# Row sums of the modulations and wide sums for the first token half of the norms, in a one-core transformer kernel

## The chip, the cores and the metric

The kernel runs on one core of one Trainium2 chip, as one launch. The metric is the time of that launch on the device in microseconds. Below, TensorE is the matmul engine (PE in the rows, with PEld for its weight loads), VectorE is DVE, ScalarE is ACT, GpSimd is POOL, and SyncE is SP. PSUM is the memory that TensorE writes to, in eight banks of 128 partitions by 512 fp32 numbers; SBUF is the memory that all else works in.

## The reference

Two blocks, one behind the other, each of depth 2, on 512 tokens of 1024 numbers. Everything is fp32.

```python
# first block, layer 0 and 1
x = x + mixer(rms_norm(x, norm_mix))             # recurrence + mLSTM, then attention in a window
x = x + conv_ffn(rms_norm(x, norm_ffn), ...)     # up 1024 -> 2 x 3072, convolution of 3 taps, gelu, down
x = x + sigmoid(rms_norm(x, norm_ple) @ gate) * (p @ proj)

# second block, layer 0 and 1
mods = (silu(c) @ ada_w[i] + ada_b[i]).reshape(B, 3, 3, D_MODEL)
h = rms_norm(x, g) * (1 + mods[:, s, 1]) + mods[:, s, 0]
x = x + 0.5 * mods[:, 0, 2] * swiglu(h)          # s = 0
x = x + mods[:, 1, 2] * mixer(h)                 # s = 1
x = x + 0.5 * mods[:, 2, 2] * swiglu(h)          # s = 2
out = rms_norm(x, final_g)

def rms_norm(x, g):
    return x * rsqrt(mean(x * x, axis=-1) + EPS) * g
```

Two things of it matter here. The modulations `mods` are a product of one row `silu(c)` with a weight of 1024 by 9216 for each of the two layers of the second block: 144 columns of 128 numbers in all. And there are 13 norms, each of which needs a sum of squares over the 1024 numbers of every token.

## The kernel before

**Layout.** The residual `X` is kept in SBUF with the 1024 numbers on eight tiles of 128 partitions and the 512 tokens along the row. A matmul in fp32 leaves two records of PE and two of PEld in the trace. The feed-forward products are done by a scheme with seven half-size products in place of eight (parts P1 to P7, each 128 partitions by 256 tokens), for which GpSimd prepares sums of weight blocks (`weight_sums_of`, four operations of 128x512 for each tile) and VectorE sums of inputs and of results. Weights come through a ring of three tiles, loaded by SP.

**What sets the order.** Each engine's instructions are written out in program order by a function of its own (`@block.tensor`, `@block.vector`, ...), with waits on semaphores between them; there is no scheduler. An engine works its list strictly from the front.

**Norms.** The norms 1 to 12 are done in two token halves (`half0` is the columns 0 to 255, `half1` the rest), so that the next product can begin on the first half while the last tile of the residual is still being updated. For each half: ScalarE squares the tiles of the residual, VectorE adds the squares of the tiles 0 to 5 into `RB` (named rstd in the rows), and the squares of the tiles 6 and 7 stay in `SQ`. `half_sum` on TensorE then uses 128x128 blocks of these squares as the stationary operand and a matrix of two columns as the moving one: six matmuls of two columns, which leave the sums of 256 tokens as two columns over 128 partitions. ScalarE takes the root of 128x2 numbers (`half_root`), VectorE the reciprocal (`half_rstd`), and `half_spread` on TensorE turns and spreads them by two matmuls of 128 columns, so that a PSUM bank holds each token's factor in all partitions. VectorE multiplies residual, gain and that bank into `H` (`half_scaled`, L2440), four tiles, then the update of the last tile, then four more. In the norms 6 to 11 ScalarE adds a shift (`shifted`). Norms 1, 4, 6, 8, 9 and 11 stand ahead of a feed-forward, 3, 7 and 10 ahead of a mixer, 2 and 5 ahead of the gate, and 12 is the last.

**Modulations.** They are computed far ahead of their use, beside the two feed-forwards of the first block (`up1`/`down1` and `up4`/`down4`, the CONVOLVED ones), 24 groups of 384 numbers in each. ScalarE's queue loads a group's weights (`ada_load`, two buffers), VectorE adds eight scaled pieces of 128x384 into a sum (`ada_half`, L2488; three buffers `ada_sum`), TensorE sums it over the partitions (`ada_group`), and VectorE adds the bias and puts three columns away (`columns`, L2463). 16 groups lie beside `up`, and eight beside `down`, two in each quarter of it.

```python
            def ada_group(g):
                pe.wait_ge(S("ada_summed"), g + 1)
                if g:
                    pe.wait_ge(S("ada_taken"), g)
                for j in range(3):
                    mm(ada_columns(g)[:, j:j + 1], ada_sum(g)[:, j * P:(j + 1) * P], const("ones")[:, 0:1], True, True,
                       S("ada_full") if j == 2 else S("ada_column"))
```

So each group is three matmuls of one column, with 128x128 of the sum as the stationary operand, and a group's product waits until the columns of the one before it were taken.

## Time and profile before

| what | value |
|---|---|
| median of 3 runs | 4083.51 us (4082.96 to 4084.88) |
| the profiled execution, its own time | 4074.79 us |
| its span, first to last instruction | 4073.0 us |
| TensorE busy | 3982.9 us, 98% of the span |
| VectorE busy | 1996.8 us, 49% |
| GpSimd busy | 1338.4 us, 33% |
| ScalarE busy | 694.1 us, 17% |
| mean granted TensorE clock | 0.993 of full |

The profiled execution is 8.7 us shorter than the median of the runs. Its durations are used below, and a difference worked out from them is taken off the median as it stands. In a timeline row the first number is the start in us from the span's start, the second the time to the end of the last of the merged instructions; the starts of neighbouring rows of one engine therefore give what a stretch costs better than the durations, since matmuls overlap.

### The profile page before, as it was taken

The page shows a single profiled execution, that of the slowest core. Times are in us where ns is not written, and L with a number is a line of the kernel's source. Part 1 is how long each engine was busy: PE and PEld are TensorE (multiplying, and loading weights), DVE is VectorE, ACT ScalarE, POOL GpSimd, SP SyncE. Part 2 cuts the span into 40 slices and gives each one's busy share as a digit, 9 for nine tenths or more (in the row PEclk, how much of TensorE's full clock was granted, in tenths as well). Part 3 has the DMA queues.
Part 4 walks back from the last instruction along what each step waited for, and adds up shares of the span by engine and source line. Part 5 has one row for each costly group of instructions (what it writes and reads, how often), then busy time and mean ns, then how long its engine had stood idle before and what let it go on. Part 6 is the DMA issues. An engine that isn't in the chain of part 4 may idle for free. (4 is left out here: it accounts for less than half of the span.)

```text
span 4073.0 us, 46434 instructions
## 1 busy us (share of the span) xinstructions
PE 3982.9 (98%) x18322; PEld 3064.3 (75%) x18322; DVE 1996.8 (49%) x3654; ACT 694.1 (17%) x1506; POOL 1338.4 (33%) x1138
## 2 busy tenths in 40 slices
PE   9999999998999999999999999999999989999999
PEld 4458888754588887888854588888888647858888
DVE  5537667448476763433245443324433754444333
ACT  2321110123211101200024310001001331221000
POOL 0004444203344341344403434444443043024443
PEclk9999999999999999999999999999999999999999
DMA  3115444210245442222210122222222132112222
GB/s 132 42 57 197 165 176 151 100 67 32 83 167 181 148 176 73 86 90 80 85 68 32 42 83 93 81 95 82 84 88 88 62 113 71 35 59 83 90 81 78
DMA packets 134216, 386.87 MB, mean 95 GB/s; under 512 B 38928, under 2 KB 47248, under 8 KB 124272
## 3 DMA queue, kind: packets, MB, share of 16 engines
q1 hardware_dynamic: 116912, 301.03, 22.5%
q10 hardware_dynamic: 16272, 79.90, 5.2%
q8 instruction: 147, 2.41, 0.2%
q0 software_dynamic: 816, 2.97, 0.2%
q14 instruction: 69, 0.57, 0.0%
HBM read 375.26 MB, written 8.39 MB: 94 GB/s over the span
## 5 line engine op out<-in xcount | busy, mean ns | idle before, releaser
L954 PE MATMUL bank<-normed,weight_ring 128*128 128x256 f32 (+1 forms) x3600 | 1012.0, 435 | 4.0 <-ACT normed L1868 1.6
L954 PEld LDWEIGHTS bank<-normed,weight_ring 128*128 128x128 f32 x3600 | 676.7, 189 | 294.3 <-issue 222.9
L954 PE MATMUL bank<-area_b,weight_ring 128*128 128x256 f32 (+3 forms) x2128 | 599.1, 429 | 5.4 <-issue 2.8
L954 PEld LDWEIGHTS bank<-area_b,weight_ring 128*128 128x128 f32 (+2 forms) x2128 | 396.4, 187 | 170.0 <-issue 125.3
L855 POOL TENSOR_TENSOR area_d<-weight_ring 128x512 f32<-128x512 f32 (+1 forms) x106 | 133.2, 1257 | 950.7 <-PE bank L954 857.7
L954 PE MATMUL bank<-area_b 128*128 128x256 f32 (+2 forms) x1656 | 364.2, 377 | 13.5 <-DVE area_b L3134 8.2
L954 PE MATMUL bank<-area_a,weight_ring 128*128 128x256 f32 (+2 forms) x1424 | 373.3, 415 | 2.2 <-DMA weight_ring<-in_weights_dram 2.2
L855 POOL TENSOR_TENSOR area_b<-weight_ring 128x512 f32<-128x512 f32 (+1 forms) x102 | 128.2, 1257 | 723.5 <-PE bank L954 638.6
L954 PE MATMUL bank<-area_b,area_d 128*128 128x256 f32 x1560 | 358.4, 381 | 5.9 <-issue 5.4
L954 PEld LDWEIGHTS bank<-area_b 128*128 128x128 f32 (+1 forms) x1656 | 299.2, 191 | 71.0 <-issue 14.8
L954 PEld LDWEIGHTS bank<-area_b,area_d 128*128 128x128 f32 x1560 | 297.0, 191 | 48.8 <-issue 6.2
L954 PEld LDWEIGHTS bank<-area_a,weight_ring 128*128 128x128 f32 (+1 forms) x1424 | 268.1, 190 | 78.8 <-issue 41.4
L954 PE MATMUL bank<-normed,area_d 128*128 128x256 f32 (+2 forms) x1568 | 312.1, 351 | 0.0
L954 PE MATMUL bank<-normed,area_b 128*128 128x256 f32 x1184 | 279.7, 379 | 0.0
L954 PEld LDWEIGHTS bank<-normed,area_d 128*128 128x128 f32 (+2 forms) x1568 | 248.2, 177 | 36.1
L1868 ACT ACTIVATE area_d<-area_d 128x512 f32<-128x512 f32 (+2 forms) x153 | 88.3, 582 | 1048.4 <-DVE area_d L2975 895.1
L954 PEld LDWEIGHTS bank<-normed,area_b 128*128 128x128 f32 x1184 | 225.0, 190 | 30.6
L1868 ACT ACTIVATE temporary<-bank 128x256 f32<-128x256 f32 (+1 forms) x196 | 80.3, 410 | 874.0 <-PE bank L954 817.1
L2606 DVE SCALAR_TENSOR_TENSOR residual<-temporary,modulations,residual 128x256 f32<-128x256 f32 x48 | 36.0, 749 | 277.3 <-ACT temporary L1868 276.5
L2488 DVE SCALAR_TENSOR_TENSOR area_b<-area_b,small_columns 128x384 f32<-128x384 f32 x224 | 163.1, 728 | 7.9
L2960 DVE TENSOR_TENSOR area_d<-temporary,bank 128x256 f32<-128x256 f32 x88 | 37.1, 421 | 252.7 <-PE bank L954 248.9
L860 POOL TENSOR_TENSOR area_d<-weight_ring,area_d 128x512 f32<-128x512 f32 (+1 forms) x106 | 152.6, 1440 | 8.3
(334 smaller groups left out, 4977.1 us busy)
## 6 DMA issues: line engine op xcount, KB each, us to landing
weight_ring<-in_weights_dram SPq DMA_DIRECT2D x429, 512.0 KB, 4.6
area_b<-in_weights_dram ACTq DMA_DIRECT2D x48, 1024.0 KB, 5.0
weight_ring<-in_weights_dram SPq DMA_DIRECT2D x27, 1024.0 KB, 4.8
area_b<-in_weights_dram ACTq DMA_DIRECT2D x48, 512.0 KB, 6.1
weight_ring<-in_weights_dram SPq DMA_DIRECT2D x43, 384.0 KB, 4.3
weight_ring<-in_weights_dram SPq DMA_DIRECT2D x29, 256.0 KB, 3.9
weight_ring<-in_weights_dram SPq DMA_DIRECT2D x38, 128.0 KB, 3.9
low_scratch<-area_d ACTq DMA_DIRECT2D x16, 256.0 KB, 2.0
```

Source lines behind the costliest of these rows:

```text
L855: po.tensor_tensor(s1, w21, w22, ALU.add).then_inc(S("pool_sum"), 1)
L860: po.tensor_tensor(s4, w12, s2, ALU.subtract).then_inc(weight_sums, 1)
L954: i = pe.matmul(out, lhsT, rhs, start=start, stop=stop)
L1868: return act.activation(out, in_, func, **kw)
L2488: i = ts(total, part, c, None, ALU.mult) if k == 0 else stt(total, part, c, total, ALU.mult, ALU.add)
L2606: return tt(x, x, part, ALU.add) if g is None else stt(x, part, g, x, ALU.mult, ALU.add)
L2960: tt(z_of(p)[:, half0], p1, part_bank("P2", p == 1), ALU.add).then_inc(part_taken, 1)
```

## The change

Two things are changed, and one follows from the first.

- **Modulation sums as rows.** A group's product is one matmul: the stationary operand is a matrix of 24 columns of which one (the group's) is ones, the moving one the whole sum of 384 columns. All 24 groups of a layer add into one region of 24 partitions by 384 columns of bank 7. At the layer's end VectorE copies it to SBUF once, TensorE turns it by three matmuls of 24 columns (`ada_turned`), and VectorE adds the bias to all 72 columns at once. `ada_taken` is gone; in its place VectorE waits, before it reuses a sum buffer, for the product of three groups before.
- **First token half of the norms.** VectorE adds the first half of tile 6's squares into `RB` too (`add_half_square`); TensorE multiplies `RB` and the squares of tile 7 by a matrix of ones (two matmuls of 256 columns), so that the sums stand in all partitions already. The root and the reciprocal are then taken on 128x256 numbers in place of 128x2, in `RB`, and `half_spread` of the first half falls away. `half_scaled` of the first half reads `RB` in SBUF in place of a PSUM bank. The second half is unchanged.
- **Groups in down.** The eight groups beside `down` are no longer summed two in each quarter, but three, three, two and none, and their products stand at other places.

```diff
+        ada_rows = bank[7][0:GROUPS, 0:3 * P]
+        ada_columns = bank[7][:, 3 * P:3 * P + 3 * GROUPS].rearrange("p (j q) -> p j q", q=GROUPS)
+        ada_copy = B[0:GROUPS, 12, 0:3 * P]
@@ TensorE
             def half_sum(n, half):
-                out = half_bank(n, half)[:, 0:2]
                 if half == 0:
                     pe.wait_ge(small_done[3], at["s"] // 4)
-                elif n in (3, 7, 10):
+                    pe.wait_ge(S("half_added"), n)
+                    mm(half_bank(n, 0)[:, half0], const("ones"), RB[:, half0], True, False)
+                    pe.wait_ge(S("half_squares"), 4 * (n - 1) + 2)
+                    slot = x_order(n).index(last_halves(n)[1][0]) % 2
+                    mm(half_bank(n, 0)[:, half0], const("ones"), SQ[:, slot, half0], False, True, S("norm_summed"))
+                    return
...
-                        if half and k == 4:
-                            half_sum(n, 0) if j == 6 else half_spread(n, 0)
+                        if half and j == 6 and k == 4:
+                            half_sum(n, 0)
...
-            def ada_group(g):
-                pe.wait_ge(S("ada_summed"), g + 1)
-                if g:
-                    pe.wait_ge(S("ada_taken"), g)
+            def ada_group(layer, g):
+                pe.wait_ge(S("ada_summed"), GROUPS * layer + g + 1)
+                own_row = C[:, CAT["group"] + GROUPS - g:CAT["group"] + 2 * GROUPS - g]
+                mm(ada_rows, own_row, ada_sum(GROUPS * layer + g), g == 0, g == GROUPS - 1, S("ada_full"))
+
+            def ada_turned(layer):
+                pe.wait_ge(S("ada_copied"), layer + 1)
                 for j in range(3):
-                    mm(ada_columns(g)[:, j:j + 1], ada_sum(g)[:, j * P:(j + 1) * P], const("ones")[:, 0:1], True, True,
-                       S("ada_full") if j == 2 else S("ada_column"))
+                    mm(ada_columns[:, j, :], ada_copy[:, j * P:(j + 1) * P], const("ident")[0:GROUPS, 0:GROUPS], True, True,
+                       S("ada_turned"))
...
-                        if conv and c == 2 and q:
-                            for e in range(2):
-                                ada_group(GROUPS * CONVOLVED.index(n) + 16 + 2 * q + e)
+                        if conv:
+                            for g in {(1, 0): (18,), (1, 2): (19, 20), (2, 0): (21,), (2, 2): (22, 23)}.get((q, c), ()):
+                                ada_group(CONVOLVED.index(n), g)
+                        if conv and (q, c) == (LAST, 1):
+                            ada_turned(CONVOLVED.index(n))
@@ ScalarE
-                a(ROOT[:, 2 * half:2 * half + 2], half_bank(n, half)[:, 0:2], ACT.Sqrt, scale=1 / 1024, bias=vec("eps", 0))\
-                    .then_inc(S("norm_root"), 1)
+                out, sums = (ROOT[:, 2:4], half_bank(n, 1)[:, 0:2]) if half else (RB[:, half0], half_bank(n, 0)[:, half0])
+                a(out, sums, ACT.Sqrt, scale=1 / 1024, bias=vec("eps", 0)).then_inc(S("norm_root"), 1)
@@ VectorE
-                dve.reciprocal(RSTD[:, 2 * half:2 * half + 2], ROOT[:, 2 * half:2 * half + 2]).then_inc(S("rstd_ready"), 1)
+                out, root = (RSTD[:, 2:4], ROOT[:, 2:4]) if half else (RB[:, half0], RB[:, half0])
+                dve.reciprocal(out, root).then_inc(S("rstd_ready"), 1)
...
                 for k in norm_order(n, half)[first:last]:
-                    stt(H[:, k, cols], X[:, k, cols], gain(n, k), half_bank(n, half)[:, cols], ALU.mult, ALU.mult)\
+                    stt(H[:, k, cols], X[:, k, cols], gain(n, k), half_bank(n, 1)[:, half1] if half else RB[:, half0],
+                        ALU.mult, ALU.mult)\
                         .then_inc(out, 1)
...
+            def add_half_square(n):
+                slot = x_order(n).index(last_halves(n)[0][0]) % 2
+                dve.wait_ge(S("half_squares"), 4 * (n - 1) + 1)
+                dve.wait_ge(S("squares_added"), 5 * (n + 1))
+                tt(RB[:, half0], RB[:, half0], SQ[:, slot, half0], ALU.add).then_inc(S("half_added"), 1)
+
+            def columns(layer):
+                own_groups = slice(GROUPS * layer, GROUPS * layer + GROUPS)
+                dve.wait_ge(S("ada_full"), GROUPS * (layer + 1))
+                dve.tensor_copy(ada_copy, ada_rows).then_inc(S("ada_copied"), 1)
+                dve.wait_ge(S("ada_turned"), 3 * (layer + 1))
+                tt(mods3[:, :, own_groups], ada_columns, bias3[:, :, own_groups], ALU.add)
...
                 if h % 2 == 0:
                     dve.wait_ge(ada_landed[g % 2], 32 * (g // 2 + 1))
+                    if g >= 3:
+                        dve.wait_ge(S("ada_full"), g - 2)
...
                 for q in range(DB // 2):
-                    for h in range(32 + 4 * q, 36 + 4 * q):
+                    for h in range(32 + 6 * q, min(38 + 6 * q, 2 * GROUPS)):
                         ada_half(layer, h)
-                    for e in range(2):
-                        columns(GROUPS * layer + 16 + 2 * q + e)
+                    if q == LAST:
+                        columns(layer)
```

The next rows are TensorE's list at norm 1, from the last tile of the first mixer's output into the first feed-forward (`project_out(1)` into `up(1)`). The rows with `rstd`, `squares` and `small_columns` are the sum and the spread; `normed,weight_ring` is the feed-forward. Before:

```order
L954 MATMUL bank<-area_b,weight_ring 128x256 x20
L954 MATMUL bank<-constant_matrices,rstd 128x2 x2
L954 MATMUL bank<-constant_matrices,squares 128x2 x4
L954 MATMUL bank<-area_b,weight_ring 128x256 x8
L954 MATMUL bank<-constant_matrices,small_columns 128x128 x2
L954 MATMUL bank<-area_b,weight_ring 128x256 x4
L954 MATMUL bank<-normed,weight_ring 128x256 x4
L954 MATMUL bank<-constant_matrices,rstd 128x2 x2
L954 MATMUL bank<-constant_matrices,squares 128x2 x4
L954 MATMUL bank<-normed,weight_ring 128x256 x4
L954 MATMUL bank<-constant_matrices,small_columns 128x128 x2
```

The same place in the changed kernel:

```order
L957 MATMUL bank<-area_b,weight_ring 128x256 x20
L957 MATMUL bank<-rstd,constant_matrices 128x256
L957 MATMUL bank<-squares,constant_matrices 128x256
L957 MATMUL bank<-area_b,weight_ring 128x256 x12
L957 MATMUL bank<-normed,weight_ring 128x256 x4
L957 MATMUL bank<-constant_matrices,rstd 128x2 x2
L957 MATMUL bank<-constant_matrices,squares 128x2 x4
L957 MATMUL bank<-normed,weight_ring 128x256 x4
L957 MATMUL bank<-constant_matrices,small_columns 128x128 x2
```

The first sum has become two matmuls of 256 columns, and the first spread is gone; the second half's sum and spread stand where they stood.

On VectorE the same place reads as follows. L2638 is the update of the residual, L2458 the sum of squares, L2432 the reciprocal, L2440 the scaling. Before:

```order
L2638 TENSOR_TENSOR residual<-residual,bank 128x256
L2458 TENSOR_TENSOR rstd<-rstd,squares 128x512
L2638 TENSOR_TENSOR residual<-residual,bank 128x256 x2
L2432 RECIPROCAL small_columns<-small_columns 128x2
L2440 SCALAR_TENSOR_TENSOR normed<-residual,vector_columns,bank 128x256 x4
L2638 TENSOR_TENSOR residual<-residual,bank 128x256
L2440 SCALAR_TENSOR_TENSOR normed<-residual,vector_columns,bank 128x256 x4
L2432 RECIPROCAL small_columns<-small_columns 128x2
L2440 SCALAR_TENSOR_TENSOR normed<-residual,vector_columns,bank 128x256 x8
```

And in the changed kernel (L2480 is the new addition, L2443 the reciprocal, L2454 the scaling):

```order
L2473 TENSOR_TENSOR rstd<-rstd,squares 128x512
L2662 TENSOR_TENSOR residual<-residual,bank 128x256
L2480 TENSOR_TENSOR rstd<-rstd,squares 128x256
L2662 TENSOR_TENSOR residual<-residual,bank 128x256
L2443 RECIPROCAL rstd<-rstd 128x256
L2454 SCALAR_TENSOR_TENSOR normed<-residual,vector_columns,rstd 128x256 x4
L2662 TENSOR_TENSOR residual<-residual,bank 128x256
L2454 SCALAR_TENSOR_TENSOR normed<-residual,vector_columns,rstd 128x256 x4
L2443 RECIPROCAL small_columns<-small_columns 128x2
L2454 SCALAR_TENSOR_TENSOR normed<-residual,vector_columns,bank 128x256 x8
```

The addition and the wide reciprocal came in, and the eight scalings of the first half read `rstd` in place of `bank`. The second half's reciprocal still stands behind the last four of them.

The last place is VectorE's list in the first quarter of `down1`, where the sums of the groups 16 and on stand (L2488, in the changed kernel L2515, eight operations a group) ahead of the quarter's results (L2606, in the changed kernel L2630). Before:

```order
L2488 TENSOR_SCALAR area_b<-area_b,small_columns 128x384
L2488 SCALAR_TENSOR_TENSOR area_b<-area_b,small_columns 128x384 x7
L2488 TENSOR_SCALAR area_d<-area_b,small_columns 128x384
L2488 SCALAR_TENSOR_TENSOR area_d<-area_b,small_columns,area_d 128x384 x7
L2463 TENSOR_TENSOR modulations<-bank,vector_columns 128x3 x2
L2606 TENSOR_TENSOR residual<-residual,temporary 128x256
L2606 TENSOR_TENSOR residual<-residual,bank 128x256
```

And in the changed kernel:

```order
L2515 TENSOR_SCALAR area_b<-area_b,small_columns 128x384
L2515 SCALAR_TENSOR_TENSOR area_b<-area_b,small_columns 128x384 x7
L2515 TENSOR_SCALAR area_d<-area_b,small_columns 128x384
L2515 SCALAR_TENSOR_TENSOR area_d<-area_b,small_columns,area_d 128x384 x7
L2515 TENSOR_SCALAR area_b<-area_b,small_columns 128x384
L2515 SCALAR_TENSOR_TENSOR area_b<-area_b,small_columns 128x384 x7
L2630 TENSOR_TENSOR residual<-residual,temporary 128x256
L2630 TENSOR_TENSOR residual<-residual,bank 128x256
```

A third group's eight operations now stand ahead of the first quarter's results.

## Rows read from the trace of the kernel before

**Rows 1.** The page: busy us, share of the span and instructions of each engine.

```profile
PE 3982.9 (98%) x18322; PEld 3064.3 (75%) x18322; DVE 1996.8 (49%) x3654; ACT 694.1 (17%) x1506; POOL 1338.4 (33%) x1138
```

**Rows 2.** Timeline at norm 1: start, us, engine, line, form, count, idle before.

```profile
302.81 0.50 PE L954 MATMUL bank<-constant_matrices,rstd 128*128 128x2 f32 x4
...
304.06 3.70 PE L954 MATMUL bank<-area_b,weight_ring 128*128 128x256 f32 x16
...
306.07 0.42 DVE L2638 TENSOR_TENSOR residual<-residual,bank 128x256 f32<-128x256 f32 x1 [4.37 <-PE bank L954]
...
307.60 0.61 PE L954 MATMUL bank<-constant_matrices,small_columns 128*128 128x128 f32 x4
...
308.05 1.89 PE L954 MATMUL bank<-area_b,weight_ring 128*128 128x256 f32 x8
...
309.77 1.89 PE L954 MATMUL bank<-normed,weight_ring 128*128 128x256 f32 x8
...
310.02 1.27 POOL L855 TENSOR_TENSOR area_d<-weight_ring 128x512 f32<-128x512 f32 x1 [115.56 <-PE bank L954]
310.31 1.65 DVE L2440 SCALAR_TENSOR_TENSOR normed<-residual,vector_columns,bank 128x256 f32<-128x256 f32 x4
...
314.57 0.61 PE L954 MATMUL bank<-constant_matrices,small_columns 128*128 128x128 f32 x4
```

**Rows 3.** Groups of instructions: form, count, busy us, mean ns, idle before.

```profile
L2868 DVE RECIPROCAL rstd<-rstd 128x512 f32<-128x512 f32 x12 | 40.2, 3352 | 34.1 <-ACT rstd L1868 34.1
...
L1868 ACT ACTIVATE temporary<-bank 128x256 f32<-128x256 f32 (+1 forms) x196 | 80.3, 410 | 874.0 <-PE bank L954 817.1
```

**Rows 4.** Lines 2440 and 2606, duration ns min/median/max, first and last start.

```profile
L2440 DVE SCALAR_TENSOR_TENSOR normed<-residual,vector_columns,bank x96: 471/476/483, 308.2 to 4069.7; 128x256 f32<-128x256 f32 x96
L2606 DVE SCALAR_TENSOR_TENSOR residual<-temporary,modulations,residual x48: 475/485/1304, 1937.4 to 4027.9; 128x256 f32<-128x256 f32 x48
```

**Rows 5.** Timeline: seven sums of a group with GpSimd idle, then beside its sums.

```profile
584.12 4.54 DVE L2488 SCALAR_TENSOR_TENSOR area_b<-area_b,small_columns 128x384 f32<-128x384 f32 x7
661.32 7.40 DVE L2488 SCALAR_TENSOR_TENSOR area_b<-area_b,small_columns 128x384 f32<-128x384 f32 x7
```

**Rows 6.** Timeline: TensorE at norm 6, GpSimd's first weight sum at norm 9.

```profile
1643.26 1.97 PE L954 MATMUL bank<-normed,weight_ring 128*128 128x256 f32 x8 [1.61 <-ACT normed L1868]
2746.89 1.27 POOL L855 TENSOR_TENSOR area_d<-weight_ring 128x512 f32<-128x512 f32 x1 [22.80 <-PE bank L954]
```

**Rows 7.** Timeline at norm 3, first half.

```profile
839.22 1.48 DVE L2458 TENSOR_TENSOR rstd<-rstd,squares 128x512 f32<-128x512 f32 x2
840.85 0.58 PE L954 MATMUL bank<-constant_matrices,rstd 128*128 128x2 f32 x4
849.84 1.65 DVE L2440 SCALAR_TENSOR_TENSOR normed<-residual,vector_columns,bank 128x256 f32<-128x256 f32 x4
```

**Rows 8.** Timeline of TensorE: a group in up1, pairs of groups in down1.

```profile
576.27 0.72 PE L954 MATMUL bank<-constant_matrices,area_b 128*128 128x1 f32 x6
576.86 3.70 PE L954 MATMUL bank<-normed,weight_ring 128*128 128x256 f32 x16
649.07 0.80 PE L954 MATMUL bank<-constant_matrices,area_d 128*128 128x1 f32 x6 [1.48 <-DVE modulations L2463]
684.31 0.72 PE L954 MATMUL bank<-constant_matrices,area_b 128*128 128x1 f32 x6
...
686.04 3.70 PE L954 MATMUL bank<-area_a,weight_ring 128*128 128x256 f32 x16
```

**Rows 9.** Waits: TensorE for the taken columns, total us, times, longest.

```profile
PE bank L954 <- DVE modulations L2463: 5.0, 8, 1.5
```

**Rows 10.** Timeline at the end of down1's first quarter; landing of the groups' loads (L1960).

```profile
651.52 0.42 DVE L2606 TENSOR_TENSOR residual<-residual,bank 128x256 f32<-128x256 f32 x1
...
660.14 3.62 PE L954 MATMUL bank<-area_a,weight_ring 128*128 128x256 f32 x16
...
DMA to landing us min/median/max: 4.7/5.0/8.5
```

More of the change, by code:

```diff
@@ L2515, in up_gelu @@
                     if p:
-                        for g in groups_after(p - 1):
-                            columns(GROUPS * layer + g)
                         taps(p - 1)
@@ L2552, in up_gelu @@
                 taps(FF1 - 1)
-                for g in groups_after(FF1 - 1):
-                    columns(GROUPS * layer + g)
                 first_sums(slice(5, 10))
```

49 lines of the change are left out of this document (26 added, 23 removed).

## The prediction

> **What bounds the kernel now.** I read the page first. TensorE is busy for 3982.9 us of a span of 4073.0, so only 90 us are idle in all, while VectorE has half its time free [rows 1]. The time is therefore TensorE's list: an edit pays by what it shortens there, and costs by the waits that it puts there. Next I read the waits, where the one that the change names, for the taken columns, is 5.0 us in 8 places [rows 9], and then the timeline around one norm [rows 2] and around the groups [rows 8]. The reader is to take the price of a stretch from the starts of neighbouring rows: sixteen records of 256 columns at 304.06 last until the next start at 307.60, 3.54 us, of which about 0.08 is a tail of the small matmuls before them, since eight such records take 1.72 us (308.05 to 309.77), or 0.216 us each [rows 2]. A matmul is two records, so one of 256 columns costs 0.43 us.
>
> **The first half's sum and spread.** Before, the sum is six matmuls, twelve records, from 302.81 to 304.06, 1.25 us, and with the 0.08 of the tail 1.33; the spread is 0.45 us (307.60 to 308.05) [rows 2]. Together 1.78 us for a norm. Now there are two matmuls of 256 columns, four records of 0.216, 0.86 us, and no spread. This removes 0.92 us from TensorE's list at each of 12 norms, 11.0 us.
>
> **What that lays on VectorE and ScalarE.** The reciprocal of 512 columns takes 3.35 us [rows 3], so one of 256 takes 1.68 in place of about 0.16. The root of 256 columns from PSUM is taken as 0.41 us, the mean of ScalarE's operations of that form [rows 3]. At norm 1 the chain is then: sum over at 303.7, root done by 304.3, update of the third half tile at 305.7 to 306.1 (306.07 less the 0.4 that the sum saves), reciprocal to 307.8, first scaled tile at 308.2. TensorE wants it at 309.77 less 0.92, 308.85 [rows 2]. It fits, since the spread's turn is gone. The same holds at norms 2, 4 and 7 to 12, where the reciprocal lies in a stretch in which VectorE waits for TensorE. It doesn't at norm 3, nor at 6, which repeats it: there the new addition comes behind two sums of squares that end at 840.70, so TensorE can start only at about 841.22, where it would have been ready at 840.75; and VectorE's second batch of scaled tiles begins at 849.7, no earlier than before, while TensorE is 0.6 us ahead [rows 7]. That costs some 0.45 and 0.3 there, 0.75 together.
>
> **The lock.** `half_scaled` read one operand in PSUM: over 96 executions it took 471 to 483 ns, whatever GpSimd did. The other line, with both tensors in SBUF, has the same median, 485 ns, but a maximum of 1304 [rows 4]. And seven sums of a group, both tensors in SBUF, take 4.54 us with GpSimd idle and 7.40 beside its weight sums [rows 5]. So such an operation waits until GpSimd's running one (1.27 us, 310.02 [rows 2]) is over. The changed scaling has both tensors in SBUF. At norm 1 GpSimd starts its weight sums the moment TensorE finishes the last half tile, and has eight operations to do in a row; VectorE's second batch of four tiles begins just then (310.31 before, 309.85 now). Each of the four will take about 1.3 us in place of 0.41, so the batch ends near 315.0. Behind it in VectorE's list stands the second half's reciprocal, and for that TensorE waits at its second spread, which it reaches at 314.57 less 0.92, 313.65 [rows 2]. Stall: about 1.35 us. Norm 4 repeats it. At norm 9 GpSimd starts at 2746.89 [rows 6], 2.7 us ahead of TensorE's first feed-forward product, so the last two tiles of the first batch are caught too: 1.4 us. At norm 6 GpSimd starts with the second batch, but TensorE itself was held by ScalarE's shift until 1643.26 [rows 6]: some 0.4. At norms 8 and 11 GpSimd is idle or late, at 2, 3, 5, 7, 10 and 12 it has no sums.
>
> The Trainium skill, "SBUF — State Buffer", section "Who interferes with whom", says that a VectorE instruction with two SBUF inputs contends with a GpSimd one that reads SBUF, the later one standing fully still until the other is over, and that one with at most one SBUF input does not. The rows agree, 483 ns against 1304; by this rule the first half's scaling is the one operation that the change moves from the free side to the locked one, and without it the norms would save about 4.5 us more.
>
> Sum for the norms: 11.0, less 0.75 each at norms 3 and 6, less 0.4 at 6, less 1.35 at 1 and 4 and 1.4 at 9, less 0.1 for small waits at 8 and 11: 11.0 - 1.5 - 0.4 - 4.1 - 0.1 = 4.9 us. At norm 6 the wait on ScalarE hides a part of the 0.75; I put 0.5 back: 5.4 us.
>
> **The groups.** Before, a group is six records from 576.27 to 576.86, 0.59 us, and 0.08 of tail, 0.67. No row has a stationary operand of 24 columns with 384 moving; its streaming is 1.5 times that of 256, two records of 0.324, 0.65 us. So 48 groups save 0.02 each, 1.0 us. The pair of groups in a quarter of down costs 684.31 to 686.04 and the tail, 1.81 us [rows 8]; two wide ones cost 1.30. Beyond the 0.02 each that is 0.47 at each of six pairs, 2.8 us, of which 5.0 - 2 x 1.48 = 2.0 is the wait for the taken columns [rows 8, 9]. At the other two pairs the wait of 1.48 is mostly for VectorE's sum of the second group, which stays; only VectorE's columns and the way back go, 0.3 each, 0.6 us. The turning adds three matmuls to each layer, at the price of a group before: 1.3 us. Sum: 1.0 + 2.8 + 0.6 - 1.3 = 3.1 us. Bounds for the unseen form: were it no dearer than 128 columns (0.45 for two, the spread), 48 groups would save 9.6 more; were it to pay an unhidden load of weights as well, at most the 0.1 of a small record for each of 96, 9.6 less. I take the streaming price, because records of 256 columns run start to start at 0.216 with their loads beneath.
>
> In the skill's page "TensorE: Matmul & The Clock Gate", section "LDWEIGHTS (loading the stationary operand)", a load takes the operand's columns divided by 1.2 in ns, 107 ns for 128 and 20 ns for 24. The trace has small records 0.104 us apart, which agrees, so the old groups and sums were bound by their loads. Its next sections hold that a load runs beside a matmul only in other rows of the array; by that each wide record of a sum would cost 0.32 and not 0.216, an estimate that takes 5 us off the gain, but the 0.216 of rows 2 speaks against it.
>
> **What moves in down.** VectorE does a third group's sum before the first quarter's results: about 7.6 us more (7.40 beside GpSimd plus the first piece). The quarter's first taken part is done at 651.52 + 0.42 = 651.9 [rows 10]; less the two small operations that fall away and with a group more it is near 658. TensorE wants it free in its second quarter, behind the first four matmuls of the sixteen records at 660.14, at 661.9 less about 1 us saved by then [rows 10]. Margin some 3 us. In the second quarter three groups of at most 7.6 us start at 662 and end by 685; TensorE issues the first two of them only at about 684.31 less 1 [rows 8], and the quarter's results come later still. The copy and the turn are waited for by VectorE alone, which has some 25 us there.
>
> **Sum.** 5.4 + 3.1 = 8.5 us off the profiled execution's 4074.79, which stands 8.7 us under the median shown; off the median it gives 4075.0 us.
>
> **Rivals.**
>
> The lock bites less: GpSimd loses the race at norm 1, 4 and 9, or the batch is through between two of its operations. For it speaks that at norm 1 its first operation starts only 0.3 us before the batch; against it the 7.40 us [rows 5], where operation after operation waited. The stalls of 4.5 us are gone: 4070.5.
>
> The lock and the long reciprocal bite more. If the second batch stalls at 6, 8 and 11 as at 1, three times another 1.2, and the wide matmuls have tails of 0.02, the gain is about 4: 4079.5. Against it speaks that GpSimd sits idle at 8 and starts late at 11.
>
> Slower than before: the third group's weights come late in the first quarter of down. VectorE stands at that group's landing, the quarter's results come late, and TensorE waits for the part in its second quarter. It costs what the landing is late beyond 3 us, twice, and eats the gain of 8.5 only from 3 + 4.3 = 7.3 us on. The load is issued when group 16's sum is done, one group's sum (some 8 us) before VectorE wants it, and landings took 4.7 to 8.5 us [rows 10], so a landing of over 15 is needed. At 10 us too late: 2 x 7 - 8.5 = +5.5, 4089.
>
> That the change doesn't do what it says is out on TensorE's side: its list shows the spread gone and the groups as one matmul. It could save nothing there only if the wide matmuls cost 0.32 a record, which would leave 3.5 us.
>
> **How the numbers follow.** Forecast 0.52, lock bites less 0.15, more stalls 0.29, late weights 0.04. A change of under 0.2%, 8.2 us, is about what a measurement of this kernel can't tell from none. The forecast lies at that bound, 4075.3, so I split it evenly with a spread of 2.5 us: faster 0.27 + 0.15 and a little of the third, 0.45; slower 0.04; within 0.2% 0.51. Range: from the light lock less a microsecond, 4069.5, to the third case and a bit, 4081.5.
>
> **What would show it.** In the changed profile: TensorE has about 16 us fewer busy in small forms and more in `rstd,constant_matrices` and 24x384; the scaling with `rstd` has a median near 480 and a maximum near 1300 ns; TensorE waits for the reciprocal of 128x2 at three norms for 1 to 1.5 us; the wait for L2463 is gone, one for the group sum of about 1.3 us stays twice. I am wrong if 24x384 is not near 0.32 us a record, if no such wait for the reciprocal appears, or if TensorE waits in the second quarter of down.

## The result, and the profile after

The changed kernel takes 4089.45 us, median of 20 runs (4082.31 to 4803.94; the last is a single disturbed run, the next below it is 4092.95), the kernel before 4080.35 (4074.68 to 4086.17, 20 runs). The ratio is 1.0019, 95% interval 1.0013 to 1.0025: 7.7 us slower, where I had forecast 8.5 us faster. The profiled execution took 4089.57 us, close to its median, while that of before, 4074.79, lies at the low end of its runs: of the 14.8 us between the two profiles about half belongs to the kernels. Busy times of the changed kernel, to be held against [rows 1]:

```profile
PE 3997.2 (98%) x17998; PEld 3029.6 (74%) x17998; DVE 2022.6 (49%) x3622; ACT 697.5 (17%) x1506; POOL 1336.3 (33%) x1138
```

TensorE has 324 records fewer and is busy 14 us longer. Its waits in the changed kernel (what was waited for, total us, times, longest):

```profile
PE bank L957 <- DVE area_b L3161: 11.6, 2, 7.9
PE bank L957 <- DVE area_b L2946: 10.7, 10, 2.2
...
PE bank L957 <- DVE small_columns L2443: 6.8, 5, 2.1
```

The wait for the taken columns [rows 9] is gone. New are 6.8 us for the second half's reciprocal (L2443), and, at a place that the prediction never looks at, 11.6 us for L3161 in the recurrent layer; before, that was 8.2 with a longest of 4.6. Norm 1 of the changed kernel, against [rows 2]:

```profile
307.04 0.59 PE L957 MATMUL bank<-rstd,constant_matrices 128*128 128x256 f32 x2
307.47 0.59 PE L957 MATMUL bank<-squares,constant_matrices 128*128 128x256 f32 x2
307.90 5.34 PE L957 MATMUL bank<-area_b,weight_ring 128*128 128x256 f32 x24
308.11 0.47 ACT L1878 ACTIVATE rstd<-bank,vector_columns 128x256 f32<-128x256 f32 x1 [1.72 <-PE bank L957]
...
310.17 1.75 DVE L2443 RECIPROCAL rstd<-rstd 128x256 f32<-128x256 f32 x1
...
313.33 1.42 POOL L858 TENSOR_TENSOR area_d<-weight_ring 128x512 f32<-128x512 f32 x1 [113.25 <-PE bank L957]
...
313.87 5.39 DVE L2454 SCALAR_TENSOR_TENSOR normed<-residual,vector_columns,rstd 128x256 f32<-128x256 f32 x4
...
319.39 0.71 PE L957 MATMUL bank<-constant_matrices,small_columns 128*128 128x128 f32 x4 [1.34 <-DVE small_columns L2443]
```

The sum takes 0.86 us (307.04 to 307.90) and the spread is gone; the second batch of four scaled tiles takes 5.39 us beside GpSimd, 1.65 before; TensorE waits 1.34. A group, alone in a feed-forward, against [rows 8]:

```profile
389.95 1.89 PE L957 MATMUL bank<-normed,area_b 128*128 128x256 f32 x8
391.77 0.83 PE L957 MATMUL bank<-area_d,constant_matrices 128*24 128x384 f32 x2
392.53 3.72 PE L957 MATMUL bank<-normed,weight_ring 128*128 128x256 f32 x16
396.08 3.62 PE L957 MATMUL bank<-area_b,area_d 128*128 128x256 f32 x16
```

From 389.95 to 396.08 are 6.13 us; 24 ordinary records of 0.216 are 5.18, so the group costs 0.95 us, not the 0.65 of the forecast. The reader should look at the neighbours too: the group begins 1.82 after eight records that elsewhere last 1.73, and the sixteen behind it last 3.55, not 3.45.

**Where the time went.** Apart from the matmuls that read constants, squares or `small_columns`, both kernels and all the variants below issue the same 16858 matmul records in the same order. The difference of the start times of the same record in two profiles, less that at the stretch's beginning, is a ledger (us later than in the profile of before). The columns are named after the experiments that follow:

| stretch | changed | rows only | norms only | 128 columns | PSUM scale | both |
|---|---|---|---|---|---|---|
| start to norm 1 | +4.2 | +4.3 | +4.1 | +4.2 | -0.3 | +4.6 |
| the two feed-forward ups, 32 groups | +9.1 | +9.1 | 0.0 | -0.8 | +9.1 | -0.8 |
| the two downs, 16 groups | -2.6 | -1.6 | -2.5 | -4.2 | -1.6 | -4.3 |
| norms 1 and 4 | -1.5 | 0.0 | -1.5 | -1.5 | -1.9 | -1.9 |
| norm 6 | +1.2 | 0.0 | +1.2 | +1.2 | -0.4 | -0.4 |
| norm 9 | +2.9 | 0.0 | +2.9 | +2.9 | -0.9 | -0.9 |
| the other eight norms | -5.9 | 0.0 | -6.0 | -5.8 | -6.0 | -5.8 |
| recurrent layer to norm 11 | +5.0 | +6.6 | -1.6 | +4.5 | +4.2 | +4.5 |
| whole | +14.8 | +21.1 | -2.5 | +0.9 | +3.8 | -2.7 |

What is missing to the whole are small stretches. The rows of the ups and the norms repeat to 0.2 us wherever the same edit is made. The first row doesn't: nothing is changed ahead of norm 1, and 4.2 us come and go between executions. The row of the downs isn't the edit's alone either: the kernel with the norms' part only has -2.5 there, with its groups as before. A part of it is that TensorE comes later to the first pair and waits 0.34 us for the taken columns in place of 1.48 [rows 8]:

```profile
651.58 0.80 PE L954 MATMUL bank<-constant_matrices,area_d 128*128 128x1 f32 x6 [0.34 <-DVE modulations L2477]
```

So the changed places give +3.2 us and the recurrent layer +5.0, together about the 7.7 of the medians. The second number is that of one execution: the profile of experiment 7, whose instructions are those of the kernel before, has +3.1 in that stretch, and its median is no longer than before's. That the two add up to 7.7 is therefore no proof that the recurrent layer costs the changed kernel 5 us.

### The profile page after: what moved, and what is told of

Its sections match the earlier page's. It is cut to its first block and busy times, and to the rows that moved or that the text cites. A ratio compares the mean times of both kernels' runs of the same rounds, so it can differ in the third digit from the quotient of the medians.

```text
span 4087.8 us, 45746 instructions
## 1 busy us (share of the span) xinstructions
PE 3997.2 (98%) x17998; PEld 3029.6 (74%) x17998; DVE 2022.6 (49%) x3622; ACT 697.5 (17%) x1506; POOL 1336.3 (33%) x1138
## 5 line engine op out<-in xcount | busy, mean ns | idle before, releaser
L957 PE MATMUL bank<-area_b 128*128 128x256 f32 (+2 forms) x1656 | 364.1, 377 | 13.3 <-DVE area_b L3161 11.6
L2630 DVE SCALAR_TENSOR_TENSOR residual<-temporary,modulations,residual 128x256 f32<-128x256 f32 x48 | 35.9, 749 | 277.3 <-ACT temporary L1878 276.5
L2515 DVE SCALAR_TENSOR_TENSOR area_b<-area_b,small_columns 128x384 f32<-128x384 f32 x224 | 156.4, 698 | 7.9
```

The costliest lines, as they stand in the source:

```text
L957: i = pe.matmul(out, lhsT, rhs, start=start, stop=stop)
L2515: i = ts(total, part, c, None, ALU.mult) if k == 0 else stt(total, part, c, total, ALU.mult, ALU.add)
L2630: return tt(x, x, part, ALU.add) if g is None else stt(x, part, g, x, ALU.mult, ALU.add)
```

## Experiments

Times below are medians, with the ratio to the kernel before from the same chip.

**1. The modulation part alone** (the kernel before, with `ada_group`, `ada_turned`, `columns` and their calls as in the change).

> The kernel before with the modulation part of the change alone (the norms' sums and spreads stay as they were). From the profile of the changed kernel a group, start of the last ordinary matmul to start of the second one behind it less two ordinary slots, takes 0.95 us where it took 0.67. Theory A (the one-matmul form itself is dear, whatever stands beside it): the 24x384 records again take 0.34 and 0.42 us start to start, each of the 32 groups in the two feed-forwards moves TensorE back by 0.28 us, 9.0 us in all, the two downs give 2.5 back, and the time is about 6.5 us over before, near 4087. Rival B (the groups are slow only because other parts of the change moved what stands around them): they fall to 0.65 us each, the wait of 5.0 us for the taken columns is gone too, and the time is about 3 us under before, 4077.

4095.62 us, ratio 1.0039 (1.0026 to 1.0051), 15.7 us over before. Theory A holds in kind, the groups cost 9.1 us in the two ups by themselves; its size is 9 us short, of which 6.6 lie in the recurrent layer and 2.6 in a stretch near 2300 us in which the granted clock is half of full (1.2 in place of 2.4 GHz), as the profile of experiment 10 has too.

**2. The norms' part alone.**

> The kernel before with the norms' part of the change alone (groups and columns as before). Read off the two profiles norm by norm, TensorE gains 0.84 us at norms 1, 2, 4, 5, 7, 9, 10, 11 and 12 and 0.67 at 8, and loses 1.3 to 1.4 at norms 1, 4 and 6 and 2.1 at 9 in waits for the second half's reciprocal. Theory A: at norms 1 and 4 that wait is given back in the first stretch of the feed-forward, where TensorE waited for VectorE anyway (1.4 us), while at norms 6 and 9 it stays and draws a half-clock stretch behind it; the sum is 1 to 2 us under before, 4078 to 4080. Rival B (the part is what I forecast, 5.4 us): 4075. Rival C (this part carries the loss): 4085 or more.

4077.36 us, ratio 0.9992 (0.9983 to 1.0001). 2.6 us under before; the interval, 7 us to none, can't tell theory A from B. The ledger can: at the norms 3.4 us are gained, with waits of 1.3 to 2.1 in them, not 5.4. C falls. At norm 1 the kernel before has, some 16 us behind the norm, this wait:

```profile
330.91 1.99 PE L954 MATMUL bank<-area_b 128*128 128x256 f32 x8 [1.38 <-DVE area_d L2529]
```

In the changed kernel some 0.2 us is left of it, since TensorE comes there later by what it stood at the norm. So the waits of norms 1 and 4 cost next to nothing.

**3. A stationary operand of 128 columns.**

```diff
-          "group": 2 * GROUPS}
+          "group": GROUPS + P}
...
-        ada_rows = bank[7][0:GROUPS, 0:3 * P]
+        ada_rows = bank[7][:, 0:3 * P]
...
-                own_row = C[:, CAT["group"] + GROUPS - g:CAT["group"] + 2 * GROUPS - g]
+                own_row = C[:, CAT["group"] + GROUPS - g:CAT["group"] + GROUPS + P - g]
...
```

> The changed kernel, with the stationary operand of a group's matmul widened from 24 to 128 columns (the added columns are zeros, so the accumulated region has 128 rows of which 24 are used; the 384 moving columns and the number of matmuls stay). Theory A (what costs is that a stationary operand of 24 columns stands between ones of 128: 0.09 us ahead of the first record, 0.09 over the streaming of the second, 0.10 behind): the records fall to 0.32 us start to start with no gap beside them, a group to 0.65, 0.30 less for each of 48, 14.4 us, and the time is about 4075. Rival B (the 384 moving columns or the accumulation of them cost it): records stay at 0.34 and 0.42, time near 4089. Rival C (a load of 128 columns is not hidden while one of 24 partly is): a group gets dearer by some 0.1 to 0.2 us, 4094 to 4099.

4076.15 us, ratio 0.9990 (0.9981 to 0.9999): 13.3 us under the changed kernel. The same group:

```profile
389.43 1.89 PE L957 MATMUL bank<-normed,area_b 128*128 128x256 f32 x8
391.16 0.81 PE L957 MATMUL bank<-area_d,constant_matrices 128*128 128x384 f32 x2
391.81 3.62 PE L957 MATMUL bank<-normed,weight_ring 128*128 128x256 f32 x16
395.26 3.62 PE L957 MATMUL bank<-area_b,area_d 128*128 128x256 f32 x16
```

5.83 us in place of 6.13: the group costs 0.65, and both neighbours have their ordinary length again. Theory A. The ledger moves by 9.9 us in the ups, 0.31 for each of 32 groups, and by 1.6 in the downs. In a down the eight groups make five visits, since three times two stand together, and such a pair pays once. That would be 3.1 us for two downs; but at the first pair of `down1` the 128-column run waits for VectorE's sum, and the changed kernel, late already, doesn't:

```profile
652.12 0.91 PE L957 MATMUL bank<-area_d,constant_matrices 128*128 128x384 f32 x2 [1.23 <-DVE area_d L2515]
```

```profile
655.95 0.83 PE L957 MATMUL bank<-area_d,constant_matrices 128*24 128x384 f32 x2
```

**4. The scaling's operand in PSUM.**

```diff
-                out, root = (RSTD[:, 2:4], ROOT[:, 2:4]) if half else (RB[:, half0], RB[:, half0])
+                out, root = (RSTD[:, 2:4], ROOT[:, 2:4]) if half else (half_bank(n, 0)[:, half0], RB[:, half0])
...
-                    stt(H[:, k, cols], X[:, k, cols], gain(n, k), half_bank(n, 1)[:, half1] if half else RB[:, half0],
+                    stt(H[:, k, cols], X[:, k, cols], gain(n, k), half_bank(n, half)[:, cols],
...
```

> The changed kernel, with the first half's reciprocal written to the norm's PSUM bank, from where the scaling reads it, so that the scaling again has one tensor in PSUM and one in SBUF; same instructions, same order. Theory A (the scaling waits for GpSimd's running operation because both of its tensors are in SBUF): its maximum falls from about 1300 ns or more to under 500, TensorE's five waits for the second half's reciprocal (6.8 us) go, and of them 1.4 and 3 us or so count, at norms 6 and 9, since at 1 and 4 a wait for VectorE in the feed-forward takes their place: about 5 us less, 4084 to 4085. Rival B (all five count): 7 us and the half-clock stretches behind them, 4080. Rival C (the waits have another cause than where the operand lies): nothing moves, 4089. The reciprocal itself should stay near 1.7 us.

4081.95 us, ratio 1.0005 (0.9997 to 1.0014), 7.5 us under the changed kernel. Scaling and reciprocal of the changed kernel, each with its mean in ns (compare [rows 4]):

```profile
L2454 DVE SCALAR_TENSOR_TENSOR normed<-residual,modulated_gains,rstd 128x256 f32<-128x256 f32 x48 | 29.8, 682 | 0.2
L2454 DVE SCALAR_TENSOR_TENSOR normed<-residual,vector_columns,rstd 128x256 f32<-128x256 f32 x48 | 27.3, 634 | 0.2
L2443 DVE RECIPROCAL rstd<-rstd 128x256 f32<-128x256 f32 x12 | 21.0, 1749 | 10.2 <-ACT rstd L1878 10.2
```

and of this one, where all 192 scalings take their factor from PSUM again:

```profile
L2454 DVE SCALAR_TENSOR_TENSOR normed<-residual,modulated_gains,bank 128x256 f32<-128x256 f32 x96 | 39.6, 475 | 9.7 <-PE bank L957 9.5
L2454 DVE SCALAR_TENSOR_TENSOR normed<-residual,vector_columns,bank 128x256 f32<-128x256 f32 x96 | 39.0, 475 | 16.3 <-PE bank L957 16.0
L2443 DVE RECIPROCAL bank<-rstd 128x256 f32<-128x256 f32 x12 | 21.1, 1757 | 10.2 <-ACT rstd L1878 10.2
```

In the changed kernel the longest scaling with `rstd` takes 1495 ns, while the second half's, whose factor stayed in PSUM, takes at most 481 in the same execution; in this one none is over 482. Waits of 1.3 to 2.1 us for L2443 are gone, and theory A's places are right: of the 7.5 us the ledger has 1.6 at norm 6 and 3.8 at norm 9, but 0.4 at 1 and 4. Norm 9 cost more than its wait of 2.14 us, since a half-clock stretch came behind it; in the profile of experiment 10, with the same wait, only 0.3 us is lost there. 25 us around it in the changed kernel (busy times of TensorE, its loads, VectorE, ScalarE and GpSimd, then the granted clock, the share and rate of the DMA):

```profile
2749.00:2774.00 25.00, 22.86 (x106) 19.70 (x106) 20.16 (x26) 10.04 (x22) 11.02 (x8) 0.93 0.24 92
```

and in this one:

```profile
2743.00:2768.00 25.00, 25.00 (x124) 21.93 (x123) 16.18 (x30) 9.69 (x22) 10.11 (x9) 1.00 0.23 91
```

**5. Which widths pay** (zeros behind the 24 used columns, the width by the group's number; a single execution, 4083.96 us).

```diff
...
+                n = P if g == GROUPS - 1 else ((P, 24, 32, 64), (P, 48, 72, 96))[layer][g % 4]
+                own_row = C[:, CAT["group"] + GROUPS - g:CAT["group"] + GROUPS + n - g]
+                mm(ada_rows[0:n, :], own_row,
...
```

> The changed kernel with stationary operands of several widths in the groups' matmuls (zeros behind the 24 used columns): by turns 128, 24, 32 and 64 columns in the first feed-forward and 128, 48, 72 and 96 in the second, 384 moving columns in all. Read from the start-to-start times around each single group in the two feed-forwards, as 0.65 us for a group without a penalty and 0.95 for the one of 24. Theory A (a tiling mode of the array that follows from the width, of at most 32, at most 64 or more columns, and a drain at each switch of mode): 24, 32, 48 and 64 all cost 0.95, 72, 96 and 128 all cost 0.65. Rival B (the cost goes with the number of columns): it falls step by step from 24 to 128. Rival C (anything short of the full 128 pays): 72 and 96 cost 0.95 too.

One group of 64 columns and one of 72, each between ordinary records:

```profile
399.65 1.89 PE L957 MATMUL bank<-normed,area_d 128*128 128x256 f32 x8
401.47 0.86 PE L957 MATMUL bank<-area_b,constant_matrices 128*64 128x384 f32 x2
402.26 3.72 PE L957 MATMUL bank<-normed,weight_ring 128*128 128x256 f32 x16
...
1181.70 1.89 PE L957 MATMUL bank<-normed,area_b 128*128 128x256 f32 x8
1183.42 0.81 PE L957 MATMUL bank<-area_d,constant_matrices 128*72 128x384 f32 x2
1184.07 3.62 PE L957 MATMUL bank<-normed,weight_ring 128*128 128x256 f32 x16
```

Start to start over the single groups, worked out as above: 24 columns 0.953 us, 32 columns 0.960, 48 columns 0.974, 64 columns 0.988; 72, 96 and 128 columns 0.645 each, all to 0.001. A step between 64 and 72, so theory A for the step, not B or C; only within the dear ones is there a slope, 0.035 us over 40 columns. The forms' mean durations:

```profile
L957 PE MATMUL bank<-area_b,constant_matrices 128*64 128x384 f32 x8 | 3.4, 512 | 0.0
...
L957 PE MATMUL bank<-area_b,constant_matrices 128*24 128x384 f32 x8 | 3.3, 494 | 0.0
...
L957 PE MATMUL bank<-area_b,constant_matrices 128*72 128x384 f32 x8 | 3.2, 486 | 0.0
```

The Trainium skill, "TensorEngine Tiling (Array Packing)", section "Tiling Modes", lists modes of 32, 64 and 128 columns and says "Mode switching requires drain". These runs agree, with 0.31 us for a visit to a narrower form and back (that it is the drain shows in no row, only its price does); the step between 64 and 72 is where that page puts the border of the 64-column mode.

**6. Both remedies.**

> The changed kernel with both remedies: 128 columns in the groups' stationary operand, and the first half's reciprocal in PSUM. Theory A (the two costs are separate and lie in separate places): they add up. Against the changed kernel's median of 4089.5 the first gave 13.3 us and the second 7.5, so 4068.7, 11 to 12 under before. Rival B (TensorE's clock or a wait behind it takes part of it back): 4072 to 4076.

4068.92 us, ratio 0.9970 (0.9958 to 0.9981), 12.6 us under before: theory A. It is faster than both kernels.

**7. The table of constants alone** (48 unused columns in the kernel before).

> The kernel before with nothing but 48 unused columns of zeros added to the table of constants in DRAM and SBUF. In the profiles of all four kernels that have the modulation part, ScalarE waits 5.7 us or so for its stores to the scratch tensor in DRAM in the recurrent layer's inner stretch (before and the norms-only kernel: 2.2 and 2.9), TensorE then waits 7.4 to 8.3 us for VectorE behind it in place of 4.6, and a second half-clock stretch follows 330 us later, 3.3 us for each. Theory A (the wider table moves what lies behind it in memory, and the stores land later for it): the same 6.6 us appear here, a time of about 4085 to 4087. Rival B (the table has nothing to do with it: chance, or the time at which the kernel comes there): as before, 4080.

4080.10 us, ratio 0.9998 (0.9989 to 1.0006), longest wait at that place 4.9 us: rival B. Its profile (4083.78 us) has +3.1 in the ledger from the recurrent layer to norm 11, of which 0.3 is that wait: this much comes and goes there with no instruction changed.

**8. Both remedies, the table as before** (`OWN = sb("own_rows", GROUPS + P)` set by two memsets).

> As the kernel with both remedies, but the group's stationary operand lies in an SBUF tensor of its own, behind all others and set by two memsets, so that the table of constants has its old width and every tensor its old place. Theory A (the wider table delays the stores of the recurrent layer): 4 to 6.6 us less than the kernel with both remedies, 4062 to 4065. Rival B: the same time as that kernel, within 1.5 us. The second memset is awaited only by the first group, 300 us later, and costs nothing.

4069.79 us, ratio 0.9970 (0.9959 to 0.9982), the long wait still there, 7.5 us: rival B. The table is out.

**9. to 11. Where the pieces of TensorE's program end.** The DMA queue q8, of kind instruction, has these rows before and after the change:

```profile
q8 instruction: 147, 2.41, 0.2%
```

```profile
q8 instruction: 144, 2.36, 0.2%
```

Each packet is 16 KB; TensorE's program leaves 37636 and 36943 records, by which an instruction is 64 bytes and a packet holds 256. The edit, with 236 or 264 waits of which two go into an instruction:

```diff
             for _ in range(5):
                 pe.matmul(bank[0][:, :], X[:, 0, 0:P], X[:, 0, :], start=True, stop=True)
+            for _ in range(236):
+                pe.wait_ge(S("x_landed0"), 16)
```

> The kernel before with 236 further waits on a semaphore that has long been there, behind the warm-up matmuls, while the matrix engine still works those off: they make its program 118 instructions longer and nothing else. What is at issue: all seven profiles of kernels with the modulation part show TensorE waiting 7.3 to 8.3 us for VectorE in the recurrent layer, at the same place where before, the norms-only and the table kernel show 4.6 to 4.9. TensorE's program is fetched in 147 (144) pieces of 16 KB, 256 instructions; the modulation part makes it 401 instructions shorter (401 = 256 + 145), both parts some 644 (512 + 132) by that place, the norms alone 243 (256 less 13). Theory A (a fetch collides with the scratch stores of that stretch, or doesn't, by where the 256-instruction pieces end): 118 more is nearly 256 less 132, so this kernel gets the long wait, 7.3 to 8.3 us, and 4 to 7 us over before, 4084 to 4087. Rival B (the modulation part delays that stretch in another way): the wait stays at 4.6 to 4.9 and the time at 4080 to 4081.

> The changed kernel with 264 such waits, 132 instructions, which bring the pieces of TensorE's program at the recurrent layer back to where they end in the kernel before. Theory A (fetches of the program): TensorE's wait there falls from 7.9 us to 4.6 to 4.9, and the time by 4 to 5 us, 4084 to 4085.5. Rival B: nothing changes, 4089.

> The kernel with both remedies (128 columns, reciprocal in PSUM) with the same 132 instructions. Theory A: 4 to 5 us under the 4068.9 of that kernel, 4064 to 4065. Rival B: 4069.

The times are 4090.13, 4095.56 and 4077.46 us (ratios 1.0025, 1.0040 and 0.9991). The waits didn't hide behind the warm-up: they kept TensorE 5.5, 6.8 and 7.4 us at the start. Less these the times are some 4084.6, 4088.8 and 4070.1: the first is what theory A said, the other two are what rival B said (4089 and 4069). The row at the place in question says more. In the kernel before:

```profile
3316.34 1.22 PE L954 MATMUL bank<-area_b 64*128 64x128 f32 x8 [4.58 <-DVE area_b L3134]
```

the kernel before, 118 instructions longer:

```profile
3330.53 1.22 PE L954 MATMUL bank<-area_b 64*128 64x128 f32 x8 [7.95 <-DVE area_b L3136]
```

the changed kernel:

```profile
3329.36 1.23 PE L957 MATMUL bank<-area_b 64*128 64x128 f32 x8 [7.93 <-DVE area_b L3161]
```

the changed kernel, 132 longer:

```profile
3336.14 1.23 PE L957 MATMUL bank<-area_b 64*128 64x128 f32 x8 [6.69 <-DVE area_b L3163]
```

both remedies, 132 longer (8.12 without):

```profile
3316.81 1.22 PE L957 MATMUL bank<-area_b 64*128 64x128 f32 x8 [4.58 <-DVE area_b L3163]
```

The wait came as theory A said in two of three; the changed kernel's went only from 7.93 to 6.69. But where it fell to 4.58, the stretch as a whole did not get shorter: from the recurrent layer to norm 11 the ledger has +5.0 in experiment 11, +4.5 in the same kernel without the instructions, and +7.2 in experiment 10.

**12. The control: one whole piece more.**

> The kernel before with 512 such waits, 256 instructions: a control for the last three runs. In them 118 instructions gave the kernel before the long wait in the recurrent layer (8.0 us), 132 took it from the kernel with both remedies (4.6), and left the changed kernel between (6.7). 256 instructions are one whole piece of TensorE's program, so the pieces end where they do in the kernel before, while the program is longer and starts later by more than in any other run. Theory A (where the pieces end decides): the wait is 4.6 to 4.9 us. Rival B (any longer program or later start brings the long wait): 7 to 8. The waits stand in TensorE's way for some 12 to 14 us at the start (118 took 5.3), which says nothing on either: the time should be 4092 to 4097 by A and 3 to 7 more by B.

4100.34 us, a single run, 22 us over the run of before beside it; TensorE stood 21.7 us at the start, and norm 1 comes 26.7 us later, twice what I had put. The recurrent layer to norm 11 differs from before by 0.03 us, and the row is:

```profile
3342.06 1.22 PE L954 MATMUL bank<-area_b 64*128 64x128 f32 x8 [4.64 <-DVE area_b L3136]
```

118 more instructions bring the long wait, 256 more don't: a longer program or a later start alone is not the cause of that wait.

## Why the prediction was wrong

**The groups' form is the step that failed.** I put "its streaming is 1.5 times that of 256, two records of 0.324, 0.65 us", and bounded the dearer side by the 0.1 us of a small record's load for each of 96 records. Measured are 0.95 us (0.645 with 72 or more columns): the streaming price was right, and a visit to the narrow form costs 0.31 on top, more than my upper bound of 0.2 for a group. At 42 visits that is 13.0 us, of which the ledger of the 128-column run shows 11.5, since a wait in down takes the rest. The prediction had named this as its first sign of being wrong: the records are 0.34 and 0.42 us apart, not 0.32.

I had bounded by the wrong neighbour, a load, though the right one stood in the trace of before, where 32 stationary columns come between 128-column matmuls of 512 and 64 columns ahead of them:

```profile
3583.10 0.67 PE L954 MATMUL bank<-normed,area_d 128*64 128x128 f32 x8
3583.70 1.98 PE L954 MATMUL bank<-per_layer_input,weight_ring 128*128 128x512 f32 x4
3585.61 0.41 PE L954 MATMUL bank<-step_squares,constant_matrices 128*32 128x128 f32 x4
3585.95 3.06 PE L954 MATMUL bank<-per_layer_input,weight_ring 128*128 128x512 f32 x12
```

The four wide records take 1.91 us; at 0.43 each, twice the 0.216 of 256 columns, they would take 1.72. So 0.2 us was lost at the two borders, as 0.09 and 0.10 are at a group's (whose own two records are 0.11 dearer besides), and a reader who subtracts starts finds it. Nor did the bound that I did work out get its due: a gain smaller by 9.6 us gives 4084.6, while the range ended at 4081.5 and no rival stood for it.

Without the dear form the ups and the downs of the 128-column run stand at -0.8 and -4.2, where I had 3.1 us gained in all; how much of the 4.2 is the groups' edit stays open, since the norms' part alone has 2.5 there.

**The sum and the spread** were right: 0.86 for 0.86 us, and 0.92 off at norms 2, 5, 7, 10 and 12. Norm 3 was nearly right: it breaks even, where I had a gain of 0.2.

**The lock** was right as a mechanism: experiment 4 takes away only the place of one operand, and waits and long scalings go. At norms 1 and 4 the wait is 1.34 us for 1.35 forecast. What it costs was wrong in both directions. At 1 and 4 a wait of 1.38 us, present before, takes it back; I had looked for what hides the edits, but not for what hides their stalls. At norm 6 I counted on TensorE being held by ScalarE's shift, and put 0.4; the whole 1.34 came, behind that hold and not in its place, and the ledger has 1.6 for it. At norm 9 it was 2.14 for 1.4, with 1.7 us lost to half clock behind it in this profile. The norms give 3.3 us in the profile (1.5 + 5.9 - 1.2 - 2.9), not 5.4; without the lock they give 9.1.

The Trainium skill, "SBUF — State Buffer", section "Who interferes with whom", was cited for this lock, and the run with the operand in PSUM agrees: 475 ns mean in place of 634 and 682.

**The recurrent layer** is not in the prediction at all. 5.0 us in the profile of the changed kernel: 3.3 is the longer wait for VectorE, which stands behind ScalarE and its stores to the scratch tensor; 3.2 is lost ahead of norm 11, and 1.6 given back near 3285. Of the 3.2, 1.5 is a longer wait for weights, in the changed kernel and before:

```profile
3649.96 14.22 PE L957 MATMUL bank<-area_b,weight_ring 128*128 128x512 f32 x37 [2.66 <-DMA weight_ring<-in_weights_dram]
```

```profile
3635.39 13.81 PE L954 MATMUL bank<-area_b,weight_ring 128*128 128x512 f32 x43 [1.14 <-DMA weight_ring<-in_weights_dram]
```

and 1.7 is half clock behind it. The stretch ahead of norm 11 in the changed kernel, granted clock in the third column from the end:

```profile
3640.00:3660.00 20.00, 17.34 (x38) 7.28 (x37) 5.17 (x8) 3.13 (x5) 2.91 (x3) 0.91 0.42 139
```

and in the kernel before:

```profile
3625.00:3645.00 20.00, 18.86 (x47) 8.52 (x46) 6.27 (x10) 3.12 (x5) 3.13 (x3) 1.00 0.40 138
```

These 3.2 us are not a consequence of the wait for VectorE: experiment 11 has the short wait and loses 3.3 us here, experiment 9 the long one and loses 0.4.

Of the wait it is shown that the modulation part's own work isn't needed (the kernel before gets it from 118 idle instructions), that the table isn't, and that 256 instructions don't bring it. Where the pieces end fits 13 of the 14 profiles (and not the 6.69). That a fetch collides with the stores at the wait is not borne out: in the kernel before, where the wait is short, a packet of q8 starts 14.8 us ahead of its end (the DMA row of q8 from 3290 to 3316 us):

```profile
q8 instruction: 1, 0.02, 0.4%
```

In the changed kernel q8 moves nothing from 27.7 us ahead of the end of the long wait until 3.0 us behind it. What is late there is one store, issued at 3317.79 and awaited until 3322.58:

```profile
3322.58 0.66 ACT L1878 ACTIVATE area_d<-bank 128x256 f32<-128x256 f32 x2 [3.07 <-DMA low_scratch<-area_d]
```

Why it is late stays open.

**What moves in down** was right in that there is no wait for the taken columns and none for the third group. The wait of 1.3 us for a group's sum, which I had kept twice, is not there: TensorE comes late by what the groups cost, and the 128-column run still has it, once. The rivals: none came. The slower one said 4089, which is the time measured; that is luck, for it was put on late weights in down, and nothing of that is seen. That the change could be slower by the form of its one new instruction was the rival I lacked. By the numbers, -8.5 forecast becomes +3.2 at the changed places by +9.6 at the groups and downs and +2.1 at the norms, and +8.1 with the recurrent layer of this one profile, against 7.7 (5.3 to 10.2) in the medians.

## What to carry to other kernels

Keep the stationary operand above 64 columns where it stands between full ones: here the added zeros cost nothing, and the narrow form costs 0.3 us a visit. A form that is new at a place has costs beside it, not only in it; look in the old trace for any narrow record among wide ones, and carry a bound that you work out into the range. Where a wide VectorE operation runs beside GpSimd, let one operand lie in PSUM. Ask of a stall not only how long it is but whether the next wait was there already. When profiles of two kernels issue the same instructions, subtract their start times: it tells at which place each microsecond is gained or lost. Hold it against a second execution of an unchanged kernel before you put a stretch down to an edit.

## What the runs showed of the chip

- A matmul of 384 columns with 24, 32, 48 or 64 stationary columns costs 0.953, 0.960, 0.974 or 0.988 us among ordinary ones, with 72, 96 or 128 it costs 0.645.
- VectorE's reciprocal writes to PSUM at the price of SBUF, 1757 against 1749 ns for 256 columns.
- TensorE's program comes in pieces of 16 KB, 144 to 148 of them in an execution. With 118 instructions more at the start, a wait 3300 us later was 7.95 us in place of 4.58, with 256 more 4.64.
- 118 and 132 instructions of satisfied waits took TensorE 5.5 and 6.8 to 7.4 us, 0.05 us each, and 256 took 21.7, though seven microseconds of matmuls were ahead of them.
- With the same instructions in the same order, one execution (experiment 7) lost 3.1 us against another (the kernel before) over one stretch of some 450 us.
